# Later key logits and late heads, memory pages turned through one bank, and four key multiplications on GpSimd, in a one-core decoder layer in float32

## The reference, cut to what matters

```python
x = x + 0.5 * swiglu_ffn(x, ffn1_norm, ffn1_w_in, ffn1_w_out)
h = rmsnorm(x, mix_norm)
proj = h @ w_in                    # u 256 | q 512 | k 512 | v 512 | qm 256 columns
y_pool, new_buf = pool_mixer(u, pool_buf, pos, pool_w, pool_scale)
q = rotary(rmsnorm(q, q_norm), pos)                # 8 heads of 64
k = rotary(rmsnorm(k, k_norm), pos)
y_moba = moba_attention(q, k_all, v_all, pos)      # prompt: causal over 256; sample: top 3 of 4 past blocks + own
y_mem = mem_attention(rmsnorm(qm, mem_q_norm), mk, mv)   # 4 heads over 256 memory tokens
x = x + concat(y_pool, y_moba, y_mem) @ w_out
x = x + 0.5 * swiglu_ffn(x, ffn2_norm, ffn2_w_in, ffn2_w_out)
```

## Time and profile before

| | us |
|---|---|
| median of 3 runs | 593.95 |
| profiled execution, device time | 594.11 |
| its span in the profile | 592.3 |
| PE busy | 570.4 (96%) |
| DVE busy | 394.4 (67%) |
| ACT busy | 264.4 (45%) |
| POOL busy | 16.1 (3%) |
| moved by DMA | 128.41 MB, mean 217 GB/s |

### The profile page before, as it was taken

One profiled execution on the slowest core, in us unless ns is written; L12 is line 12 of the kernel. 1 busy time (PEld: TensorE's weight loads), 2 busy tenths in 40 slices (PEclk: granted clock), 3 DMA queues, 4 the chain that ended last, 5 costly groups with the idle time before them and its releaser, 6 DMA issues.

```text
span 592.3 us, 13485 instructions
## 1 busy us (share of the span) xinstructions
PE 570.4 (96%) x5104; PEld 522.7 (88%) x5104; DVE 394.4 (67%) x707; ACT 264.4 (45%) x420; POOL 16.1 (3%) x24
## 2 busy tenths in 40 slices
PE   9999999999999999988899968999999999999997
PEld 7999999999899997655576746989999999999997
DVE  4776767768688876996654443488777776774443
ACT  5834345354543345433354654564343434353331
POOL 1000000000000003000000000040000000000000
PEclk9999999999999999998999989999999999999999
DMA  8799988775677638897999925446666666575522
GB/s 220 215 261 296 257 260 239 221 228 191 224 237 240 224 107 293 312 386 269 328 330 308 352 72 182 117 127 185 179 177 177 177 177 177 177 242 184 177 71 74
DMA packets 133121, 128.41 MB, mean 217 GB/s; under 512 B 6624, under 2 KB 103991, under 8 KB 133071
## 3 DMA queue, kind: packets, MB, share of 16 engines
q1 hardware_dynamic: 132791, 127.76, 68.5%
q10 hardware_dynamic: 288, 0.08, 0.1%
HBM read 125.12 MB, written 2.83 MB: 216 GB/s over the span
## 4 chain that ended last, share of the span: by engine, by line
PE 75%; DVE 11%; issue 5%; ACT 5%; DMA 2%; SPq 1%; DVEq 0%; ACTq 0%
PE banks L1451 21%; PE banks L1453 20%; PE banks L1452 20%; PE banks L1459 4%; DVE w_lo L976 3%; ACT w_hi L679 3%; PE banks L1860 2%; DVE kv L987 2%; PE banks L1590 2%; DMA raw<-in_w_in 1%; PE banks L1781 1%; PE banks L1560 1%; DVE h_tmp L1022 1%; DVE h_tmp L1017 1%; DVE sg L1012 1%
## 5 line engine op out<-in xcount | busy, mean ns | idle before, releaser
L976 DVE TENSOR_TENSOR w_lo<-raw,w_hi 128x1024 fp32r<-128x1024 f32 x158 | 193.3, 1230 | 107.7 <-ACT w_hi L679 106.3
L1451 PE MATMUL banks<-x_hi,w_hi 128*128 128x264 f32 x768 | 221.4, 288 | 2.5 <-DVE h_tmp L1017 0.9
L1452 PE MATMUL banks<-x_lo,w_hi 128*128 128x264 f32 x768 | 218.0, 284 | 0.0
L1453 PE MATMUL banks<-x_hi,w_lo 128*128 128x264 f32 x768 | 217.9, 284 | 0.0
L679 ACT ACTIVATE w_hi<-raw 128x1024 fp32r<-128x1024 f32 x158 | 161.8, 1050 | 89.3 <-PE banks L1453 76.0
L1451 PEld LDWEIGHTS banks<-x_hi,w_hi 128*128 128x128 f32 x768 | 145.0, 189 | 5.8 <-issue 2.2
L1452 PEld LDWEIGHTS banks<-x_lo,w_hi 128*128 128x128 f32 x768 | 145.2, 189 | 0.0
L1453 PEld LDWEIGHTS banks<-x_hi,w_lo 128*128 128x128 f32 x768 | 144.4, 188 | 0.0
L1451 PE MATMUL banks<-h_hi,w_hi 128*128 (+1 forms) x352 | 100.2, 285 | 0.0
L1453 PE MATMUL banks<-h_hi,w_lo 128*128 (+1 forms) x352 | 100.2, 285 | 0.0
L1452 PE MATMUL banks<-h_lo,w_hi 128*128 (+1 forms) x352 | 100.0, 284 | 0.0
(11 more groups left out here) (280 smaller groups left out, 505.4 us busy)
## 6 DMA issues: line engine op xcount, KB each, us to landing
raw<-in_ffn_w_in SPq DMA_DIRECT2D x86, 512.0 KB, 4.3
raw<-in_ffn_w_out SPq DMA_DIRECT2D x44, 512.0 KB, 3.4
kv<-in_cache_k SPq DMA_DIRECT2D x56, 256.0 KB, 4.8
kv<-in_cache_v SPq DMA_DIRECT2D x48, 256.0 KB, 5.0
raw<-in_w_in SPq DMA_DIRECT2D x12, 512.0 KB, 6.3
late_slot<-in_cache_v SPq DMA_DIRECT2D x16, 256.0 KB, 4.6
raw<-in_w_out SPq DMA_DIRECT2D x8, 512.0 KB, 5.8
raw<-in_mem_w_kv SPq DMA_DIRECT2D x4, 512.0 KB, 3.3
```

The costliest lines, as they stand in the source:

```text
L976: vec.tensor_tensor(w_lo[:, n % RING, :], raw[:, n % RING, :], w_hi[:, n % RING, :].bitcast(F32), ALU.subtract).then_inc(lo_ready, 1)
L1451: pe.matmul(out, lhs[0], rhs[0], start=start, stop=False)
L1452: pe.matmul(out, lhs[0], rhs[1], start=False, stop=False)
L1453: return pe.matmul(out, lhs[1], rhs[0], start=False, stop=stop)
```

## The change: what it does

- Key logits K 0 to K 7 stand later in the order (K 0 and 1 from ahead of part 0 of round 3 to ahead of part 1, K 6 from round 6 to round 7, K 7 from round 7 to round 8). S 4 to S 7 stand together behind them in round 3. A 0 to A 5, NS 4 and NG 4, V 0 to V 3 and all heads stand later, by up to two rounds. A 3 stands at the head of round 10, where it stood at the head of round 9. W 11 stays placed by hand and W 12 to W 15 stay where `steps()` puts them.
- Memory pages 0 to 3 are turned in round 15, the others between steps of the tail. All use bank 6, and each waits for the one before to be evacuated. Pair 5 of the heads waits for all pages (bank 6) and for the second pooling output (bank 5), PV 4 for the first (bank 4).
- The last four projection rounds take their units in the order 1, 2, 3, 0 in place of 2, 3, 0, 1.
- The four multiplications of the prompt's keys run on GpSimd, between DVE's reciprocal (NS 4) and rotary step (NG 4), where DVE waits for them.
- SP reads the page numbers of batch 6 ahead of the memory keys, and those of batch 7 behind value batch 5.
- The first unit of the second feed-forward layer multiplies all tiles of `x_hi` first (waiting for each), then those of `x_lo`; the second unit has no waits of its own.

```diff
-HY_BANKS, POOL_BANKS, MK_BANKS, QM_BANK = (6, 3, 4), (4, 5), (6, 5, 4), 7
+HY_BANKS, POOL_BANKS, MK_BANK, QM_BANK = (6, 3, 4), (4, 5), 6, 7
-J_ORDER = (2, 3, 0, 1)
+J_ORDER = (2, 3, 0, 1) * 3 + (1, 2, 3, 0)
...
+            2: {1: [("QT", 0), ("WL", 3)], 4: [("QT", 2), ("SS", 0), ("WL", 4)]},
+            3: {0: [("WL", 5), ("NV", 1)], 1: [("K", 0), ("K", 1), ("ND", 1), ("NS", 1), ("WL", 6), ("G", 16), ("G", 17), ("G", 18), ("G", 19)],
+                2: [("K", 2), ("K", 3), ("QF", 1)], 3: [("S", 4), ("S", 5), ("S", 6), ("S", 7), ("ES", 1), ("ET", 0)], 4: [("ET", 1)]},
+            4: {0: [("NQ", 2), ("G", 20), ("G", 21)], 1: [("NR", 2)], 2: [("K", 4), ("G", 22), ("G", 23)], 3: [("NV", 2), ("NQ", 3)],
                 4: [("ND", 2), ("NS", 2), ("WL", 7), ("G", 24)]},
+            5: {1: [("T", 0), ("NV", 3), ("ND", 3), ("G", 25)], 2: [("K", 5), ("G", 26)], 3: [("T", 1)], 4: [("G", 27), ("NS", 3), ("WL", 8)]},
+            6: {0: [("NG", 3)], 1: [("G", 28)], 2: [("G", 29)], 3: [("WL", 9), ("G", 30)], 4: [("S", 8)]},
+            7: {1: [("G", 31)], 2: [("K", 6)], 3: [("ET", 2)], 4: [("S", 9), ("ET", 3), ("NQ", 4), ("WL", 10), ("W", 11)]},
+            8: {0: [("OWN", 0)], 2: [("NV", 4), ("ND", 4)], 3: [("K", 7)], 4: [("S", 10), ("A", 0), ("OWN", 1)]},
+            9: {0: [("WL", 11)], 1: [("A", 1)], 2: [("A", 2), ("S", 11), ("ES", 2)], 4: [("WL", 12)]},
+            10: {0: [("NS", 4), ("A", 3)], 3: [("NG", 4)]},
+            11: {2: [("A", 4)], 3: [("ET", 4)], 4: [("ET", 5), ("S", 12), ("WL", 13)]},
+            12: {1: [("A", 5), ("T", 2)], 2: [("T", 3)], 3: [("V", 0)], 4: [("HA", 0), ("HM", 0), ("HM", 1), ("HE", 0), ("HE", 1), ("S", 13)]},
+            13: {0: [("V", 1), ("WL", 14)], 2: [("HV", 0), ("HV", 1)], 3: [("HB", 0), ("HT", 0), ("HB", 1), ("HT", 1)],
+                 4: [("PV", 0), ("V", 2), ("HA", 1), ("HM", 2), ("HM", 3), ("HE", 2), ("HE", 3), ("S", 14)]},
+            14: {0: [("WL", 15)], 2: [("HV", 2), ("HV", 3)], 3: [("V", 3), ("HB", 2), ("HT", 2), ("HB", 3), ("HT", 3)],
+                 4: [("S", 15), ("ES", 3), ("PV", 1), ("HA", 2), ("HM", 4), ("HM", 5), ("HE", 4), ("HE", 5), ("HY", 0), ("YR", 0)]},
+            15: {0: [("X", 0), ("W", 16)], 1: [("MG", 0), ("Y", 0), ("HV", 4), ("HV", 5)], 2: [("MG", 1), ("HB", 4), ("HT", 4), ("HB", 5), ("HT", 5)],
+                 3: [("MG", 2), ("ET", 6), ("NQ", 5), ("WL", 16)],
+                 4: [("PV", 2), ("HA", 3), ("HM", 6), ("HM", 7), ("HE", 6), ("HE", 7), ("ET", 7), ("NV", 5), ("MG", 3), ("V", 4)]},
+        TAIL = ([("T", 4), ("NQ", 6), ("HV", 6), ("HV", 7), ("POOL", 0), ("MG", 4), ("HB", 6), ("HT", 6), ("HB", 7), ("HT", 7), ("NV", 6), ("ND", 5), ("ND", 6),
+                 ("NS", 5), ("NS", 6), ("MG", 5), ("PV", 3), ("HA", 4), ("HM", 8), ("HM", 9), ("POOL", 1), ("MG", 6), ("HE", 8), ("HE", 9),
+                 ("QT", 1), ("V", 5), ("MG", 7), ("HV", 8), ("HV", 9), ("HA", 5), ("HM", 10), ("HM", 11), ("HY", 1), ("W", 17), ("HB", 8), ("HT", 8),
+                 ("HB", 9), ("HT", 9), ("HE", 10), ("HE", 11), ("MK", 0), ("M", 0), ("WL", 17), ("V", 6), ("HV", 10), ("HV", 11), ("PV", 4), ("M", 1),
+                 ("HB", 10), ("HT", 10), ("HB", 11), ("HT", 11), ("M", 2), ("W", 18), ("V", "mem"), ("YR", 1), ("PV", 5), ("HY", 2), ("WL", 18), ("V", 7), ("Y", 1),
...
+            keep_pages(6)
             load_memory("mk")
-            keep_pages(6)
+            load_batch("v", 5)
             keep_pages(7)
-            load_batch("v", 5)
...
+            pool.wait_ge(rs_ready, 1)
+            heads = kp[:].rearrange("p t (h d) -> p t h d", d=HD)
+            for t in range(2):
+                pool.tensor_tensor(heads[:, t], heads[:, t], rs_h[:, t * MH:(t + 1) * MH].unsqueeze(2).to_broadcast([P, MH, HD]), ALU.mult)\
+                    .then_inc(kp_scaled, 1)
...
+                elif what == "NS" and k == 4:
+                    vec.wait_ge(sd_ready, 5)
+                    vec.reciprocal(rs_h[:], sd_h[:, 0, 0:16]).then_inc(rs_ready, 1)
...
+                    if k == 4:
+                        vec.wait_ge(kp_scaled, 4)
...
+                if k_at is not None:
...
+                    for idx, k in enumerate(order):
+                        pe.wait_ge(xhi_ready, k_at + idx + 1)
+                        pe.matmul(out, w(k)[0], x_hi[:, k, :], start=(idx == 0), stop=False)
+                        pe.matmul(out, w(k)[1], x_hi[:, k, :], start=False, stop=False)
+                    for idx, k in enumerate(order):
                         pe.wait_ge(xlo_ready, k_at + idx + 1)
+                        mm = pe.matmul(out, w(k)[0], x_lo[:, k, :], start=False, stop=(idx == KT - 1))
```

More of the change, by code:

```diff
@@ L272, in layer @@
         s_stats, s_shared, s_sums = sem("s_stats"), sem("s_shared"), sem("s_sums")
-        k_turned, kT_ready = [sem(f"k_turned{i}") for i in range(3)], [sem(f"kT_ready{i}") for i in range(3)]
+        k_turned, kT_ready = sem("k_turned"), sem("kT_ready")
         q_turned, mk_used = sem("q_turned"), sem("mk_used")
@@ L346, in mem_page @@
             return slots[SLOT_OF["mk", 0]][:, b * 512:(b + 1) * 512]
-        def mem_last(bank_):
-            return len([b for b in range(NS) if MK_BANKS[b % 3] == bank_])
         def key_pair(g):
@@ L388, in layer @@
             1: {2: [("S", 0), ("S", 1), ("S", 2), ("S", 3), ("ES", 0), ("NQ", 1), ("W", 3), ("NR", 1)], 4: [("W", 4)]},
[22 rows of a table removed]
-        }
-        TAIL = ([("HY", 0), ("T", 4), ("NQ", 6), ("POOL", 0), ("HY", 1), ("NV", 6), ("ND", 5), ("ND", 6), ("NS", 5), ("NS", 6), ("MG", 0), ("HA", 4), ("POOL", 1), ("W", 17),
-                 ("HM", 8), ("HM", 9), ("QT", 1), ("V", 5), ("WL", 17), ("MG", 1), ("MG", 2), ("MG", 3), ("HE", 8), ("HE", 9)] +
-                [("MG", b) for b in range(4, 8)] +
[3 rows of a table removed]
-                 ("CAT", 0), ("YR", 2), ("MIX", 0), ("MIX", 1), ("Y", 2), ("CAT", 1), ("MIX", 2), ("MX", 0), ("MX", 1), ("MX", 2), ("MIX", 3)])
[20 rows of a table added]
+        }
+        TAIL = ([("T", 4), ("NQ", 6), ("HV", 6), ("HV", 7), ("POOL", 0), ("MG", 4), ("HB", 6), ("HT", 6), ("HB", 7), ("HT", 7), ("NV", 6), ("ND", 5), ("ND", 6),
[5 rows of a table added]
         placed = [token for extra in EXTRA.values() for tokens in extra.values() for token in tokens if token[0] == "W"] +\
@@ L658, in _ @@
                 pool.tensor_tensor(tmp[:, M_ORDER[a_], :], tmp[:, M_ORDER[a_], :], tmp[:, M_ORDER[b_], :], ALU.add).then_inc(sum_step, 1)
+            pool.wait_ge(rs_ready, 1)
[3 more added lines that the diff above has]
+                    .then_inc(kp_scaled, 1)
+            for t in range(2):
+                pool.wait_ge(kp_scaled, t + 1)
+                pool.tensor_tensor(heads[:, t], heads[:, t], head_gain[:, 0, :].unsqueeze(1).to_broadcast([P, MH, HD]), ALU.mult)\
+                    .then_inc(kp_scaled, 1)
             pool.wait_ge(sc_ready, MH)
@@ L697, in key_evac @@
             def key_evac(b):
-                act.wait_ge(k_turned[b % 3], b // 3 + 1)
-                act.activation(mem_page(b), bank[MK_BANKS[b % 3]][:, :], ACT.Copy).then_inc(kT_ready[b % 3], 1)
+                act.wait_ge(k_turned, b + 1)
+                act.activation(mem_page(b), bank[MK_BANK][:, :], ACT.Copy).then_inc(kT_ready, 1)
             def silu(f, c, s):
@@ L979, in key_evac @@
             def key_evac(b):
-                vec.wait_ge(k_turned[b % 3], b // 3 + 1)
-                vec.tensor_copy(mem_page(b), bank[MK_BANKS[b % 3]][:, :]).then_inc(kT_ready[b % 3], 1)
+                vec.wait_ge(k_turned, b + 1)
+                vec.tensor_copy(mem_page(b), bank[MK_BANK][:, :]).then_inc(kT_ready, 1)
             def turn_pair(g):
@@ L1315, in _ @@
                 elif what == "NG":
-                    chain(heads_gain(*ropes[k][0:3], 0))
+                    if k == 4:
+                        vec.wait_ge(kp_scaled, 4)
+                    else:
+                        chain(heads_gain(*ropes[k][0:3], 0))
                     heads_rope(*ropes[k])
@@ L1464, in ffn_unit @@
                 pe.wait_ge(lo_ready, i * 4 + (n + 1))
-                for idx, k in enumerate((range(KT), M_ORDER)[f]):
-                    if k_at is not None:
+                order = (range(KT), M_ORDER)[f]
+                if k_at is not None:
+                    w = lambda k: weights(n % RING, k * P, (k + 1) * P)
+                    out = bank[b0 + j][:, 0:N]
+                    for idx, k in enumerate(order):
[3 more added lines that the diff above has]
+                    for idx, k in enumerate(order):
                         pe.wait_ge(xlo_ready, k_at + idx + 1)
+                        mm = pe.matmul(out, w(k)[0], x_lo[:, k, :], start=False, stop=(idx == KT - 1))
+                for idx, k in enumerate(order if k_at is None else ()):
                     mm = three(bank[b0 + j][:, 0:N], weights(n % RING, k * P, (k + 1) * P),
@@ L1568, in key_turns @@
                     pe.wait_ge(hy_lo, 1)
-                elif b < 3:
-                    pe.wait_ge(pool_lo, 2)
                 else:
```

(9 more changed lines are left out.)

15 lines of the change are left out of this document (8 added, 7 removed), and 25 rows, old and new, of tables (EXTRA, TAIL).

## The result

The changed kernel takes 604.74 us (median of 4 runs, 603.89 to 606.65) against 593.61 us (4 runs, 592.88 to 594.25) for the kernel before, run beside it: a ratio of 1.0192, 95% interval 1.0163 to 1.0222. It is slower, by 11.1 us. The profiled execution took 603.89 us, 9.78 more than that of before; its span is 602.1 us.

The account below looks back on a forecast made before the run. PE was taken as the bound, losing time between 250 and 366 us, with SP's unbroken issuing a second bound. 7.3 + (9.4 − 9.2) + 0.25 = 7.75 on 594.11, less 0.16: 601.7 us; range 594.5 to 606.5.

Parts of the forecast that it names:

- the rival with the lower clock: After idling, PE starts at 1.2 GHz; two later places cost 1.65 us each, giving 605 us; chance 0.10.
- The early gains: Up to A 4, PE's waits of 4.7, 0.7 and 2.8 us and K 7's 1.65 clock loss would go.
- A 3 behind unit 13: On ACT the exponentials wait for unit 13, landing at 289.9; A 4 at 293.9, PE idle 12 us.
- W 14 ahead of ET 4: On ACT, unit 14's split delays ET 4; round 12 starts at 300.2, PE waits 3 us more.
- How far behind that is: At round 12, PE stands 7.3 us behind the kernel before, counting work the old order had done.
- The tail: Rounds 12 to 15 and tail: waits sum to 9.4 us against 9.2 before, MG 0's new 3.4 included.
- Waits much under 9: Sign that the prediction is wrong: the tail's waits sum to much under 9 us.
- Second feed-forward layer: At its first unit, ten matmuls instead of three follow the last tile: +0.25 us.
- GpSimd: Key multiplications take 1.59 us each, 6.4 for four, hidden by the late exponentials of A 3.
- The case without cover: Without the late exponentials hiding GpSimd, DVE would hold back A 4's part and A 5 by some 3 us.
- The exponentials are not held: Faster rival: unit 13 lands by 281, so A 3 is not delayed; 588.2 us; chance 0.10.
- The tail takes it up: Even rival: the tail's waits shrink from 9.4 to 2.5 us, giving 594.9 us; chance 0.10.

Follow-up runs that it names:

- e1: The changed kernel with only A 3's exponentials moved ahead of ACT's split of unit 13: 607.02 us, ratio 1.0176.
- e2: e1 with ACT's splits of units 13, 14 and 15 placed later, behind ET 5, HE 1 and HT 1: 595.54 us, ratio 1.0005.
- e3: The changed kernel with SP's loads of units 12 to 15 issued ahead of value batches 2 and 3, ACT's order untouched: 597.6 us, ratio 1.0023.
- e4: The changed kernel with the four multiplications of the prompt's keys back on DVE: 605.02 us, ratio 1.0148.
- f4: e2 with HY 0 directly behind PV 1, the second feed-forward layer's old first unit, and A 3 also ahead of unit 12's split: 596.57 us.
- h1: The changed kernel with e1's edit, HY 0 and YR 0 behind PV 1, the old first feed-forward unit, and units 12 to 14 loaded earlier: 585.21 us.
- h2: h1 with the four multiplications of the prompt's keys back on DVE: 586.56 us, ratio 0.9851.

## Why the prediction was right

The mechanism was right: two late units at the head of ACT's queue, and most of the loss, 7.2 of 9.75 us, in place when round 12 starts. The size was 3.0 us short. The measured 604.74 lies in the stated range of 594.5 to 606.5, but 0.7 above the forecast's own range of 597.5 to 604, and next to the rival with the lower clock (605).

- *The early gains.* Right. K 6 and K 7 ran without waits and at the full clock; PE stood at A 4 at 280.74, forecast 282.
- *A 3 behind unit 13.* Right, in place and size: unit 13's split ended at 291.1 (landing forecast 289.9, measured 290.1), A 4 at 294.2 (293.9), PE idle for 13.4 (12). e1 and e2 show it by removing it: A 4 moved to 283.7 and 284.6. That the landing came out to 0.2 us is in part luck. Unit 8 was issued at 243.48 and not 244.5, SP took 41.1 us from there to unit 13 and not 39.9, and the landing followed after 5.5 us and not 6.45.
- *W 14 ahead of ET 4.* Right: round 12 at 300.50 (300.2), and e1 shows it as a second gate that alone holds the whole loss. PE's own wait there was 1.2 and not 3, since it worked at 1.2 GHz between A 4 and round 12; this is the stretch that the rival of the clock had called hidden, and it was. SP was the source of both late landings, as said; e3 shows that by its order of issue.
- *How far behind that is.* Forecast 7.3. From round 12 to MIX 0 before took 65.11 us, with 6.9 of waits and 1.7 lost to the lower clock: 56.5 of work. After: 74.82, with 7.7 of waits and 3.4 lost: 63.7. The difference is 7.2.
- *The tail.* The forecast had +0.2; it is +2.5: waits 7.7 against 6.9 (+0.8) and lower clock 3.4 against 1.7 (+1.7). Here the sum was off, in three ways. MG 0's 3.4 was right (3.5, in e2 too). Of the small waits at MG 1 and HB 4, PV 3 and HB 8, 2.15 us together, only 0.3 came. And the sum of 9.4 for after held no lower clock and no loss at the pooling heads, while the 9.2 for before held both, 1.6 and 0.7: the two sides were not counted alike. The lower clock stood among the rivals with 0.10, at two places with 1.65 each; it came at two places, MG 0 and V mem, with 1.7 each. The first of these was named in the prediction, the second was not: so the rival's 605 is near the measured time for half the reason that it gave. The term that was mis-sized is thus the tail, +0.2 forecast and +2.5 measured. "Waits much under 9" stood among the prediction's signs of being wrong, and 7.7 came near that.
- *Second feed-forward layer.* Forecast +0.25, measured +0.05.
- *GpSimd.* Forecast 1.59 each and hidden; 1.02 and 1.24, and hidden (e4). The case without cover was also right in kind: f4 and h1 show DVE held 4.6 us in NG 4 and A 5 waiting behind it.
- *The total.* 7.3 + 0.2 + 0.25 = 7.75 forecast, 7.2 + 2.5 + 0.05 = 9.75 found, on the profiled executions 9.78. The rest of the distance from 601.7 to 604.7 is that this profiled execution lies 0.85 under its median, where that of before lay 0.16 above: 3.0 us, of which 2.0 are the terms and 1.0 the two medians. The kernel before had higher medians beside the experiments (594.94 to 595.5 and not 593.61): e4, which is as slow as the changed kernel, lies 9.7 above the 595.35 beside it, so the loss is 10 to 11 us.
- *The rivals.* "The exponentials are not held" would have given 588.2, deciding on unit 13 by 281. h1 makes just that true, with MG 0's wait down to 1.7 and no lower clock besides, and takes 585.2. e2 and e3, which open one side each, ended at 595.5 and 597.6: units that came late still held A 4 (unit 12 by 3.7 us in e2, 12 and 13 by 6.7 in e3), and the clock fell in three places in each. The rival's price was near, its condition too narrow. "The tail takes it up" did not happen: MG 0's wait is 3.5 wherever PE stands (after, e1 to e4).
- *Small slips.* The even case is 601.7 − 6.9 = 594.8, not 594.9; 392.9 + 10 x 0.122 is 394.12, not 394.15; the 1.9 called V 1 is the row of V 0 (V 1 at 298.60 took the same 1.93); and from A 4 at 293.9 the prediction's own numbers leave PE 3.7 us of waiting ahead of round 12, not 3. None changes the sum.

Still open is how much of the even result of e2 to f4 is the clock. In each of their profiles PE is at 1.2 GHz in two or three stretches of 3.4 to 7 us, and their runs spread over 3 to 6 us where h1's spread over 1.3; but h2's spread over 4. No run changed the clock without changing waits.

## What to carry to other kernels

A step moved past an entry in an in-order queue inherits that entry's latest producer: before a reordering, list for each engine what stands ahead of the moved step and when that is fed, back to the queue that issues the loads. Where compute is pulled forward, pull its loads forward with it and measure both together: here the order alone cost 10 to 11 us, the loads alone brought nothing that could be measured, and both with the small repairs brought 10. Count what else stands in the queue that issues the loads: here it was 4.5 us of reading page numbers, with the DMA idle at their end. When waits are summed for two versions, count the same kinds of loss on both sides, the clock included.
